# Weight loads of 512 KB, each with a slot and a semaphore of its own, in a two-layer decoder kernel

## What is computed

```python
for layer in range(DEPTH):                      # 2
    h = rmsnorm(x, norm_mix[layer])
    x = x + (even_mixer if layer % 2 == 0 else conv_mixer)(h, ...)
    h = rmsnorm(x, norm_ffn[layer])
    # top-1 group, then top-2 experts in it; for each of 16 experts:
    #   out += combine[:, e] * ((silu(t @ w_gate[e]) * (t @ w_up[e])) @ w_down[e])
    x = x + hier_moe(h, ...)
return rmsnorm(x, norm_final)
```

## Time and profile before

| | before |
|---|---|
| median of three runs | 1117.73 us |
| the profiled execution: its own time, and its span | 1120.8 us, 1119.1 us |
| PE busy | 1088.3 us, 97% of the span |
| DVE busy | 877.2 us, 78% |
| ACT busy | 666.7 us, 60% |
| weight loads of 1 MB by SP | 226 (w_gate 64, w_up 64, w_down 64, mixers 34) |
| bytes moved | 285.89 MB, mean 255 GB/s |

### The profile page before, as it was taken

How to read it: one execution, slowest core, us unless ns; L and a number is a source line. 1 busy time by engine, 2 the same in 40 slices (tenths; PEclk the granted TensorE clock), 3 DMA queues, 4 the chain that set the end, 5 groups by cost and what they waited for, 6 DMA issues and landing times.

```text
span 1119.1 us, 15254 instructions
## 1 busy us (share of the span) xinstructions
PE 1088.3 (97%) x5353; PEld 821.1 (73%) x5353; DVE 877.2 (78%) x1138; ACT 666.7 (60%) x846; POOL 104.2 (9%) x159
## 2 busy tenths in 40 slices
PE   7999999999999999999999999999999999999996
PEld 5777777678867777777776888878877777777772
DVE  5256765787699999999999453644599999999997
ACT  5224444523488888888876413222388888888872
POOL 2010000212110000000012000000110000000022
PEclk9999999999899999999999999999899999999998
DMA  9742222212389999999999422332189999999985
GB/s 323 200 142 76 85 85 76 89 44 76 114 295 396 405 394 394 409 395 410 404 364 344 143 82 76 113 108 81 76 284 394 406 393 397 406 397 410 405 334 196
DMA packets 78643, 285.89 MB, mean 255 GB/s; under 512 B 17687, under 2 KB 17687, under 8 KB 62204
## 3 DMA queue, kind: packets, MB, share of 16 engines
q1 hardware_dynamic: 66396, 241.64, 56.6%
q0 software_dynamic: 8464, 30.42, 8.2%
q10 hardware_dynamic: 3728, 13.11, 2.9%
HBM read 266.27 MB, written 20.20 MB: 256 GB/s over the span
## 4 chain that ended last, share of the span: by engine, by line
PE 88%; DVE 6%; ACT 2%; DMA 1%; issue 1%; POOL 1%; DVEq 0%; POOLq 0%; SPq 0%; ACTq 0%
PE ps L1814 26%; PE ps L1816 25%; PE ps L1815 25%; PE ps L2147 2%; PE ps L2061 1%; DVE w_split L1052 1%; PE ps L2083 1%; ACT w_split L657 1%; PE ps L1789 1%; PE ps L1898 1%; PE ps L2171 1%; PE ps L2012 1%; PE ps L2246 1%; DMA arena<-h_rows_dram,arena 1%; PE ps L1919 1%
## 5 line engine op out<-in xcount | busy, mean ns | idle before, releaser
L1052 DVE TENSOR_TENSOR w_split<-ring,w_split 128x1024 fp32r<-128x1024 f32 x428 | 511.1, 1220 | 43.8 <-ACT w_split L657 32.6
L657 ACT CAST w_split<-ring 128x1024 fp32r<-128x1024 f32 x428 | 446.3, 1052 | 127.5 <-PE ps L1816 125.3
L1814 PE MATMUL ps<-w_split,hT 128*96 128x512 f32 (+2 forms) x976 | 386.0, 396 | 5.3 <-DVE hT L1560 1.7
L1816 PE MATMUL ps<-w_split,hT 128*96 128x512 f32 (+2 forms) x976 | 379.4, 389 | 0.0
L1815 PE MATMUL ps<-w_split,hT 128*96 128x512 f32 (+2 forms) x976 | 378.9, 388 | 0.0
L1814 PEld LDWEIGHTS ps<-w_split,hT 128*96 128x96 f32 (+1 forms) x976 | 163.0, 167 | 66.3 <-issue 3.6
L1816 PEld LDWEIGHTS ps<-w_split,hT 128*96 128x96 f32 (+1 forms) x976 | 162.9, 167 | 60.0
L1815 PEld LDWEIGHTS ps<-w_split,hT 128*96 128x96 f32 (+1 forms) x976 | 163.2, 167 | 53.8
L1814 PE MATMUL ps<-hT,w_split 128*128 128x512 f32 (+1 forms) x384 | 144.8, 377 | 2.3 <-DVE hT L1088 1.0
L1815 PE MATMUL ps<-hT,w_split 128*128 128x512 f32 (+1 forms) x384 | 142.8, 372 | 0.0
L1816 PE MATMUL ps<-hT,w_split 128*128 128x512 f32 (+1 forms) x384 | 142.7, 372 | 0.0
(11 more groups left out here) (266 smaller groups left out, 919.6 us busy)
## 6 DMA issues: line engine op xcount, KB each, us to landing
ring<-in_exp_w_gate SPq DMA_DIRECT2D x64, 1024.0 KB, 11.9
ring<-in_exp_w_up SPq DMA_DIRECT2D x64, 1024.0 KB, 11.6
ring<-in_exp_w_down SPq DMA_DIRECT2D x64, 1024.0 KB, 12.7
ring<-in_w_in_even SPq DMA_DIRECT2D x14, 1024.0 KB, 9.7
y_rows_dram<-arena ACTq DMA_DIRECT2D x32, 384.0 KB, 7.0
ring<-in_w_in_odd SPq DMA_DIRECT2D x12, 1024.0 KB, 7.5
ring<-in_w_out_even SPq DMA_DIRECT2D x4, 1024.0 KB, 4.9
h_rows_dram<-arena POOLq DMA_DIRECT2D x8, 512.0 KB, 3.2
```

The lines of the kernel that those rows point to most:

```text
L657: ins = s.copy(hi_of(c), raw(c))
L1052: ins = v.tensor_tensor(lo_of(c), raw(c), hi_of(c).bitcast(F32), ALU.subtract)
L1814: mm(out, a[0], b[0], start=start, stop=False)
L1816: return mm(out, a[0], b[1], start=False, stop=stop)
```

## The change

`load` issues one DMA per chunk instead of one per two chunks: four of 512 KB for a piece. The ring is the same memory, now read as 12 slots of one chunk; there are 12 `slot_landed` semaphores, ACT waits for the one of its chunk, and SP waits on `lo_ready` for the chunk that lay in the slot, one chunk at a time. A load of gate or up weights then has runs of 4 KB; the runs of the others stay as they are. To have six semaphores more, some that are used once are merged: `gates_hi` and `lam_exp` into `gate_act`, `vbias_full`, `gates_full` and `gate_cols_full` into `bias_gates_full`, `lam_sum` and `subln_ready` into `subln_lam`, and `v_copied` into `v_stored`. The waits on them get the counts of their place in the order.

```diff
-        slot_landed = [sem(f"slot_landed{i}") for i in range(RING)]
+        slot_landed = [sem(f"slot_landed{i}") for i in range(2 * RING)]
...
-                rows = src.shape[1] // 2
-                for half in halves:
-                    n = 2 * piece + half
-                    if n >= RING:
-
-                        sp.wait_ge(lo_ready, plus(2 * (n - RING) + 2, i, 24))
-                    sp.dma_start(ring[:, n % RING, :].rearrange("p (k n) -> p k n", k=rows),
-                                 src[:, half * rows:(half + 1) * rows, :]).then_inc(slot_landed[n % RING], 16)
+                rows = src.shape[1] // PIECE
+                for part in range(PIECE // 2 * halves[0], PIECE // 2 * (halves[-1] + 1)):
+                    c = PIECE * piece + part
+                    if c >= 2 * RING:
+
+                        sp.wait_ge(lo_ready, plus(c - 2 * RING + 1, i, 24))
+                    sp.dma_start(raw(c).rearrange("p (k n) -> p k n", k=rows),
+                                 src[:, part * rows:(part + 1) * rows, :]).then_inc(slot_landed[c % (2 * RING)], 16)
...
-                    n = c // 2
-                    act.wait_ge(slot_landed[n % RING], plus(16 * (n // RING + 1), i, 32))
+                    act.wait_ge(slot_landed[c % (2 * RING)], plus(16 * (c // (2 * RING) + 1), i, 32))
...
-            s.copy(w_gates_split[:, 0, :, :], w_gates[:, :, :]).then_inc(gates_hi, 1)
+            s.copy(w_gates_split[:, 0, :, :], w_gates[:, :, :]).then_inc(gate_act, 1)
...
-            act.wait_ge(lam_sum, 2)
-            s.activation(st[:, 10:12], st[:, 8:10], ACT.Exp).then_inc(lam_exp, 1)
+            act.wait_ge(subln_lam, 3)
+            s.activation(st[:, 10:12], st[:, 8:10], ACT.Exp).then_inc(gate_act, 1)
...
-            pe.wait_ge(gate_act, 2)
+            pe.wait_ge(gate_act, 4)
```

More of the change, by code:

```diff
@@ L199, in hybrid_trunk @@
         consts_ready, zeros_ready = sem("consts_ready"), sem("zeros_ready")
-        slot_landed = [sem(f"slot_landed{i}") for i in range(RING)]
+        slot_landed = [sem(f"slot_landed{i}") for i in range(2 * RING)]
         hi_ready, lo_ready = sem("hi_ready"), sem("lo_ready")
         chunk_done = sem("chunk_done")
-        gates_hi, gates_split = sem("gates_hi"), sem("gates_split")
+        gates_split = sem("gates_split")
         cat_hi, cat_split = sem("cat_hi"), sem("cat_split")
-        vbias_full, v_row_ready, v_stored = sem("vbias_full"), sem("v_row_ready"), sem("v_stored")
-        v_copied = sem("v_copied")
+        v_row_ready, v_stored = sem("v_row_ready"), sem("v_stored")
         bias_loaded = [sem("bias_loaded0"), sem("bias_loaded1")]
-        gates_full, gate_cols_full = sem("gates_full"), sem("gate_cols_full")
+        bias_gates_full = sem("bias_gates_full")
         gate_act, gate_rows_ready, gate_cols_ready = sem("gate_act"), sem("gate_rows_ready"), sem("gate_cols_ready")
         job_full, job_act, job_dve = sem("job_full"), sem("job_act"), sem("job_dve")
-        lam_sum, lam_exp, subln_ready = sem("lam_sum"), sem("lam_exp"), sem("subln_ready")
+        subln_lam = sem("subln_lam")
         o_unit = sem("o_unit")
@@ L557, in _ @@
             for h in range(HEADS):
-                pool.dma_start(v_rows_dram[h], v_dram[h].unsqueeze(0).broadcast_to([P, VROW])).then_inc(v_copied, 16)
-            pool.wait_ge(v_copied, 16 * HEADS)
+                pool.dma_start(v_rows_dram[h], v_dram[h].unsqueeze(0).broadcast_to([P, VROW])).then_inc(v_stored, 16)
+            pool.wait_ge(v_stored, 16 + 16 * HEADS)
             load_bias(0)
@@ L817, in scale_out @@
                 act.wait_ge(on_turned, h + 1)
-                act.wait_ge(subln_ready, 1)
+                act.wait_ge(subln_lam, 1)
                 s.activation(q_cat[:, HEADS + h, :], ps[:, out_turn_bank(h), :], ACT.Copy,
@@ L1118, in _ @@
             for half in range(2):
-                dve.wait_ge(vbias_full, half + 1)
+                dve.wait_ge(bias_gates_full, half + 1)
                 last = v.tensor_copy(v_row[0:HEADS, half * 320:half * 320 + 320], ps[0:HEADS, 4 + half, 0:320])
@@ L1122, in _ @@
             splits(at_last_job(1))
-            dve.wait_ge(gates_hi, 1)
+            dve.wait_ge(gate_act, 1)
             v.tensor_tensor(w_gates_split[:, 1, :, :], w_gates[:, :, :], w_gates_split[:, 0, :, :].bitcast(F32),
@@ L1129, in _ @@
             dve.wait_ge(small_loaded, 16 * SMALL)
-            v.tensor_scalar(subln[:, :], subln[:, :], 1.0 - LAM_INIT, None, ALU.mult).then_inc(subln_ready, 1)
+            v.tensor_scalar(subln[:, :], subln[:, :], 1.0 - LAM_INIT, None, ALU.mult).then_inc(subln_lam, 1)
             for i in range(2):
                 link(v.tensor_tensor(lams[:, 2 * i, :], lams[:, 2 * i, :], lams[:, 2 * i + 1, :], ALU.mult))
-                v.tensor_reduce(st[:, 8 + i:9 + i], lams[:, 2 * i, :], AX, ALU.add).then_inc(lam_sum, 1)
-            dve.wait_ge(lam_exp, 1)
+                v.tensor_reduce(st[:, 8 + i:9 + i], lams[:, 2 * i, :], AX, ALU.add).then_inc(subln_lam, 1)
+            dve.wait_ge(gate_act, 2)
             link(v.tensor_tensor(st[:, 12:13], st[:, 10:11], st[:, 11:12], ALU.subtract))
@@ L1137, in _ @@
             lam = st[:, 13:14]
-            dve.wait_ge(gates_full, 1)
+            dve.wait_ge(bias_gates_full, 3)
             G = lambda k: gate_rows[0:HEADS, k, :]
@@ L1148, in _ @@
             job(9)
-            dve.wait_ge(gate_act, 1)
+            dve.wait_ge(gate_act, 3)
             link(v.tensor_tensor(f, f, soft_part, ALU.subtract))
@@ L1160, in _ @@
             splits(at_start(3))
-            dve.wait_ge(gate_cols_full, 1)
+            dve.wait_ge(bias_gates_full, 4)
             v.tensor_copy(st[:, 32:64], ps[:, 1, 0:32]).then_inc(gate_cols_ready, 1)
@@ L1867, in _ @@
                 mm(ps[0:HEADS, 4 + half, 0:320], rel_w[0:BUCKETS + 1, :],
-                   table[0:BUCKETS + 1, half * 320:half * 320 + 320], start=True, stop=True).then_inc(vbias_full, 1)
+                   table[0:BUCKETS + 1, half * 320:half * 320 + 320], start=True, stop=True).then_inc(bias_gates_full, 1)
             all_jobs(range(6, 8))
@@ L1874, in _ @@
                            (hT[:, 0, k, :], hT[:, 1, k, :]), k == 0, k == KD - 1)
-            last.then_inc(gates_full, 1)
+            last.then_inc(bias_gates_full, 1)
             all_jobs(range(8, EARLY))
-            pe.wait_ge(gate_act, 2)
+            pe.wait_ge(gate_act, 4)
             pe.wait_ge(gate_rows_ready, 2)
@@ L1884, in _ @@
                                                ident[0:HEADS, 0:HEADS])
-            last.then_inc(gate_cols_full, 1)
+            last.then_inc(bias_gates_full, 1)
             keep_busy(11, 3)
```

## The result

The change costs 4.6 to 5 us. That is small, but above what the measurement leaves open. The forecast of 1117.7 us stood on the median of three runs; over 20 runs the kernel before has 1115.69, 2 us less, and the loss counts from there.

What follows compares the result with a forecast made beforehand. The prediction took PE to bound the kernel, with the DMA engines a hair behind. Its terms, 0 + 0 + 0, left the profiled 1120.8 us unchanged, 1117.7 us on the median; the range was 1115.8 to 1124.0 us.

Steps and rivals of the forecast that it cites:

- rival A: Last experts of each layer: DMA engines become the bound if gate and up loads move under 408 GB/s; chance 0.16.
- The rate and the cost per step: Expert stage: gate and up loads at 412 GB/s cost 0.26 us a step, so the stream loses 0.35 us per expert.
- reserve 3: Start of the expert stage: the first load waits for one chunk instead of two, putting 1.3 us of transfer ahead.
- reserve (2): Expert stage: a chunk no longer waits for its neighbour's half of the transfer, so it lands 1.3 us earlier.
- What covers it: Expert stage: reserves of 5.9 us in all against a loss of 4.6, so PE never waits and the cost is 0.
- the 2.2 us: Expert steps: PE's reserve once ACT and DVE are late, up to the matmuls needing the next tokens' low part.
- the one DMA on the path: First gather of each layer: bounds of -0.5 to +1.3 us per layer, taken as 0.
- B: All loads: a fixed cost per transfer shows, 0.1 us for each of six more a step giving 1124 us; chance 0.02.
- C: First gather of each layer: both layers at -0.5 us give 1116.7, both at +1.3 give 1120.3; late end's chance 0.01.
- E: Whole kernel: faster by more than 2 us, through something unseen behind PE's idle time; chance 0.07.
- D: SP's queue takes no more loads than before, reserve 3 is gone, time stays; chance within the forecast's 0.74.
- the semaphores: Merged semaphores: raised in their engine's program order with the same waits ahead, no work added, cost 0.

Runs made afterwards that it cites:

- e10: The changed kernel with the last quarter of each loop step's down weights cut to 64 columns in layer 0 only; 3.5 us behind the kernel before.
- e6: The kernel before with each 1 MB load issued as two of 512 KB, even and odd partitions, runs of 8 KB kept; 1115.56 us, ratio 0.9989.
- e8: The kernel before with the loads of the last 12 chunks of layer 1 cut to 64 columns; 1117.18 us, ratio 0.9996.
- e12: The kernel before with the last quarter of the down weights left out of each loop step in both layers; its time is not in the text.
- e13: The kernel before with only the change's merged semaphores, loads as before; 1116.61 us against 1116.83, ratio 0.9992.
- e3: The kernel before with each 1 MB load issued as two of 512 KB, one per half of the partitions, runs of 8 KB kept; 1434.36 us.
- e2: The kernel before with ring chunks set 32 bytes apart, giving 4 KB runs in the experts' 1 MB transfers; 1125.99 us, ratio 1.0089.

## Why the prediction was wrong

The time of 1120.67 us lies inside the stated range, which was wide enough for rival A and stood on a base 2 us too high. The forecast itself was no change, and the change costs 4.6 to 5 us.

- **The rate and the cost per step: right.** 411 GB/s for 412, and 17.92 us between late landings, 0.35 over PE's 17.57.
- **The first load earlier (reserve 3): real, and gone at once.** The stage's first loads go out at 306.89 and 309.19 us, where the earlier trace rows have 311.65. PE is 2.5 us ahead of the kernel before by then, from the clock; net of that the first goes out 2.3 us before the load of the earlier trace rows, as forecast, and the second with it:

```profile
306.89 2.63 SPq L313 DMA_DIRECT2D ring<-in_exp_w_up  x2
311.28 3.73 SPq L313 DMA_DIRECT2D ring<-in_exp_w_down  x4
```

  The first chunk of the first expert's down weights lands at 337.62 us, 3.7 us before ScalarE splits it. That is the lead that the prediction summed. The same chunk of the next experts lands 19.65, 18.22 and 17.84 us after the one before. So at the load of the earlier trace rows, where the prediction counted on 3.7 us, 1.7 were left, 0.5 more than the kernel before has there. The lead was made while the DMA engines had little to do, and one step later it was 2 us smaller; no run tells reserve (2) from (3) in this. ScalarE waits for weights steadily from 428 us on, after six steps and not ten.
- **The step that failed is the last of "What covers it": "PE never waits. The cost is 0."** The sum had 4.6 us of loss against 5.9 of reserve, with 1.3 to spare. From the load of the earlier trace rows on it was 1.7 + 2.2 = 3.9 us of reserve against 12 steps at 0.35, 4.2. Against PE's own pace the load of the earlier trace rows lands 2.4 us later than in the kernel before, where 0.2 us of slack were left. That uses up the 2.2 us: PE waits 0.7 us for VectorE behind the last loop step and is 0.9 to 1.2 us late by then in each layer. It waits there for the hidden rows of the last expert but one and their turned copy, not for the tokens' low part, for which the 2.2 us were worked out. A margin of 1.3 us hung on a reserve that was wrong by 2.
- **What it never priced** is the other half, 1.6 to 2.1 of the 4 us: what else is on the DMA engines when a late stream ends. The prediction asked only whether weights reach PE in time. At the end of layer 1 the results must be stored and gathered, behind the last weights; these end 4.3 us later against the store, the store takes 6.9 us instead of 3.9, and PE waits 1.8 (2.9 in e10). Nor is the first gather "the one DMA on the path": the second fetch of x at 221 us is on it too, and an earlier gate load makes it late (0.3 us of PE in this trace).
- **The rivals.** A was the right place and mechanism (the end of each layer, the DMA engines the longer stream), but its threshold of 408 GB/s, which stood on the same reserve, was wrong: the loss is 4.6 to 5 us at 411. B fell (e6). C did not come: PE's turn at the first gather starts 0.7 us earlier in layer 0 (net of the clock), and the 0.52 us of the earlier trace rows are gone. Some 0.3 us of that is that one trace's, as e8, e12 and e13, whose loads there are the kernel before's, start 0.3 us earlier too. E did not come. D is false, since loads went out earlier; the semaphores cost 0 (e13).

## What to carry over

When two resources run within 2% of each other, slowing the hidden one is free only until its reserve runs out: follow the late stream to its end and list all that queues behind it there, the stores and gathers too. A lead gained while the DMA engines were idle was all but gone one step later here, so don't count it for the stage without a row that shows it kept. A finer slot also lets a load out earlier, in front of some small transfer that is on the path. To split a transfer without cost, keep its contiguous runs: here halving the transfer was free and halving the run was not.

## What the runs showed of the hardware

Transfers over one half of the partitions ran at about 0.6 of the rate. e3 and e6 have the same packets and the same bytes, and differ only in which partitions a transfer covers. First e3, then e6:

```profile
q1 hardware_dynamic: 70012, 241.66, 70.4%
...
ring<-in_exp_w_gate SPq DMA_DIRECT2D x128, 512.0 KB, 22.2
```

```profile
q1 hardware_dynamic: 70012, 241.66, 56.4%
...
ring<-in_exp_w_gate SPq DMA_DIRECT2D x128, 512.0 KB, 10.7
```

In e3 the median 8 KB packet took 552 ns (309 in e6), and the expert stages moved some 245 GB/s in place of 400. The Trainium skill has this: by "SBUF — State Buffer", section "Door 1: The DMA port swizzle", partitions 0 to 63 reach 8 of SBUF's 16 DMA ports, and 64 to 127 reach the other 8; by its formula the even partitions reach all 16. The measurement goes the same way, and 245 GB/s is a little above the 218 that the page gives for 8 ports.

The address of an operand can set the pace of matmuls: with the tensors behind the ring 384 bytes further on (e2) an expert's step is 0.6% longer, at the same granted clock. No run here shows which operand it is.

The median packet of 4 KB took 164 ns and that of 8 KB 311 ns in the kernel before, 41 and 39 ns per KB. With weight loads alone the rate was 411 GB/s in the new runs and 423 in the old ones, 3% less, and that was enough.
